# Expert layer of a two-layer encoder: each group's highest expert last, and half of the experts' rows read back during the last two blocks

## The reference

```python
xn = rms_norm(x, norm1)
[q|k|v|q_idx|k_idx|w_idx|u|v_s|g_a|g_b] = xn @ W_in
h = x + (sigmoid(g_a) * (attention @ w_pa) + sigmoid(g_b) * (sgu @ w_pb)) @ w_out
# hier_moe(rms_norm(h)): 4 groups of 8 experts, hidden width 128
g_w, g_idx = top_k(softmax(xf @ w_rg + b_rg), 1)           # one group per token
e_w, e_idx = top_k(softmax(logits of that group), 2)       # two experts in the group
out = sum over the two experts of gate * ((silu(xf @ w_eg) * (xf @ w_eu)) @ w_ed)
y = h + out                                                # next layer, or the final RMSNorm
```

## Time and profile before

| | |
|---|---|
| runs, median (lowest to highest) | 1464.19 us (1463.33 to 1464.4) |
| the profiled execution's own time | 1469.72 us |
| its span in the trace | 1468.0 us |
| PE busy | 1323.0 us, 90% |
| DVE busy | 541.5 us, 37% |
| ACT / POOL busy | 342.6 us, 23% / 219.7 us, 15% |
| DMA moved | 205.63 MB, mean 140 GB/s |
| mean granted TensorE clock | 0.952 |

### The profile page before, as it was taken

One profiled execution on the slowest core, in us unless ns is written; L12 is line 12 of the kernel. 1 busy time (PEld: TensorE's weight loads), 2 busy tenths in 40 slices (PEclk: granted clock), 3 DMA queues, 4 the chain that ended last, 5 costly groups with the idle time before them and its releaser, 6 DMA issues.

```text
span 1468.0 us, 15494 instructions
## 1 busy us (share of the span) xinstructions
PE 1323.0 (90%) x5756; PEld 733.9 (50%) x5756; DVE 541.5 (37%) x1542; ACT 342.6 (23%) x773; POOL 219.7 (15%) x304
## 2 busy tenths in 40 slices
PE   7999898999999996998599989899999999979790
PEld 5654345544444555655385544464444445556450
DVE  1278885100111236321244779831011103452115
ACT  2232466200000100222213325651000010112121
POOL 5011033000000001223240200600000000013313
PEclk9999999999999997999799999999999999979895
DMA  8302102502403316799571110042060060279966
GB/s 237 115 13 59 58 1 70 172 0 70 145 0 121 152 43 227 300 407 392 206 203 58 50 47 34 8 131 104 0 215 0 0 258 29 86 279 410 405 261 237
DMA packets 95485, 205.63 MB, mean 140 GB/s; under 512 B 26465, under 2 KB 35905, under 8 KB 95409
## 3 DMA queue, kind: packets, MB, share of 16 engines
q1 hardware_dynamic: 80800, 178.13, 34.3%
q0 software_dynamic: 14608, 26.49, 5.1%
HBM read 196.29 MB, written 27.78 MB: 153 GB/s over the span
## 4 chain that ended last, share of the span: by engine, by line
PE 81%; DVE 5%; issue 4%; ACT 4%; DMA 3%; PEld 2%; PEldq 1%; POOL 0%; SPq 0%; POOLq 0%; ACTq 0%; DVEq 0%
PE bank L747 34%; PE bank L1029 9%; PE bank L1080 9%; PE bank L1126 8%; PE bank L1137 4%; PE bank L780 3%; PE bank L1113 2%; DMA uv<-xd,mb 2%; PE bank L829 1%; DVE stat L1687 1%; PE bank L1046 1%; PE bank L733 1%; PE bank L933 1%; PE bank L833 1%; DVE x L1821 1%
## 5 line engine op out<-in xcount | busy, mean ns | idle before, releaser
L747 PE MATMUL bank<-ring,xt 128*128 128x512 f32 (+1 forms) x1120 | 434.6, 545 | 7.5 <-DMA ring<-in_w_in 4.5
L747 PEld LDWEIGHTS bank<-ring,xt 128*128 128x128 f32 x1120 | 214.6, 194 | 209.5 <-issue 189.8
L1756 DVE TENSOR_TENSOR scr<-scr,bank 128x512 f32<-128x512 f32 x20 | 13.8, 688 | 368.8 <-PE bank L1029 368.8
L1080 PE MATMUL bank<-ring,xt 128*128 128x512 f32 x320 | 141.3, 594 | 0.0
L541 POOL TENSOR_SCALAR stat<-stat 128x1 f32<-128x1 f32 (+1 forms) x27 | 10.3, 381 | 805.8 <-ACT uv L1213 617.0
L1357 ACT ACTIVATE scr<-bank,stat 128x512 f32<-128x512 f32 x40 | 25.3, 684 | 348.0 <-PE bank L747 348.0
L1080 PEld LDWEIGHTS bank<-ring,xt 128*128 128x128 f32 x320 | 59.3, 190 | 67.0 <-issue 67.0
L780 PE MATMUL bank<-ring,xt 128*128 128x512 f32 x160 | 75.9, 608 | 0.0
L1029 PE MATMUL bank<-ring,att 128*128 128x512 f32 x160 | 72.5, 596 | 2.2 <-ACT sgt L1349 1.8
L1029 PE MATMUL bank<-ring,sgt 128*128 128x512 f32 x160 | 71.9, 592 | 0.0
L747 PE MATMUL bank<-more,xt 128*128 128x512 f32 x160 | 70.3, 592 | 0.0
(11 more groups left out here) (285 smaller groups left out, 1848.7 us busy)
## 6 DMA issues: line engine op xcount, KB each, us to landing
ring<-in_w_in SPq DMA_DIRECT2D x12, 2048.0 KB, 9.2
ring<-in_w_ed SPq DMA_DIRECT2D x32, 512.0 KB, 16.7
ring<-in_w_eg SPq DMA_DIRECT2D x26, 512.0 KB, 10.8
ring<-in_w_eu SPq DMA_DIRECT2D x26, 512.0 KB, 16.8
ring<-in_w_out SPq DMA_DIRECT2D x4, 2048.0 KB, 12.5
more<-in_w_ed SPq DMA_DIRECT2D x14, 512.0 KB, 9.7
qkv<-in_w_eg SPq DMA_DIRECT2D x12, 512.0 KB, 6.3
qkv<-in_w_eu SPq DMA_DIRECT2D x12, 512.0 KB, 7.7
```

The lines of the kernel that those rows point to most:

```text
L747: mm = pe.matmul(out, xt[:, k, t * P:(t + 1) * P], rhs[:, k, :], start=(k == 0), stop=(k == KD - 1))
L1080: mm = pe.matmul(banks[5 + n % 3][:, :], xt[:, k, t * P:(t + 1) * P], w[:, k, :], start=(k == 0), stop=(k == KD - 1))
```

## The change

The experts are renumbered for the blocks: 28 of them (the first seven of each group) in order, then the four that are the highest of their groups. These four fill the last two blocks, b = 15 and 16, and so these blocks write no row of half k = 1. That half is complete once the scatter of block 14 has landed.

SP therefore waits for the scatters of blocks 0 to 14 only, reads half k = 1 (5 DMAs of 512 KB, into the space of `qkv`), then handles the branch for further rows, waits for all scatters, and reads half k = 0 (5 DMAs). DVE adds half k = 1 to x within the blocks' loop: tiles 0 and 1 after `hidden_rows` of block 15, tiles 2 to 4 after that of block 16 (`first_of`). `combine` then has one operation for each tile.

Two further edits belong to it: once, in the first layer, POOL copies the inputs over half k = 1 of `yd` (DRAM to DRAM, 2.6 MB), and waits for that before the first gather; and the final norm's gain is loaded to another place. Only the core of the diff is shown.

```diff
+REST_AT = (0, 8)
+EXPERT_OF = [e for e in range(EXPERTS) if e % NE < NE - 1] + [e for e in range(EXPERTS) if e % NE == NE - 1]
...
-        fin_gain = qkv_flat[:, 2048:2048 + D]
+        fin_gain = more[:, 3072:3072 + D]
...
-        pairs = [w.rearrange("p (k c) -> p k c", k=2) for w in
-                 (uv_flat[:, 0:2048], uv_flat[:, 2048:4096], sgt_flat[:, 512:2560], more[:, 0:2048], more[:, 2048:4096])]
+        last_rows = [uv_flat[:, D * t:D * t + D] for t in range(PT)] + [more[:, 0:D]]
+        first_rows = [qkv[:, t, 0:D] for t in range(NT)]
...
@@ SP, behind the last load of expert weights
+                if L + 1 < DEPTH:
+                    sp.wait_ge(y_psum[L], RING_FREE)
+                    key_columns(L + 1)
+                else:
+                    sp.wait_ge(y_psum[L], RING_FREE)
+                    sp.dma_start(fin_gain, a["final_norm"].partition_broadcast(P)).then_inc(s_gain, 16)
+                by_pair = yd.rearrange("(k t p) c -> k t p c", k=2, t=NT)
+                for z in range(YBUF):
+                    sp.wait_ge(y_out[z], scatters(z) * L + 16 * len(range(z, OVER_AT + 1, YBUF)))
+                for t in range(NT):
+                    sp.dma_start(first_rows[t], by_pair[1, t]).then_inc(combine_in[t][1], 16)
                 sp.wait_ge(experts_known, prior("experts_known", L) + 1)
                 with sp.If(sp.value_load(over_count[:, 0:1], min_val=0, max_val=OVER) != 0):
...
                 for z in range(YBUF):
                     sp.wait_ge(y_out[z], scatters(z) * L + scatters(z))
                 for t in range(NT):
-                    for k in range(2):
-                        sp.dma_start(pairs[t][:, k, :], yd.rearrange("(k t p) c -> t k p c", k=2, t=NT)[t, k]
-                                     ).then_inc(combine_in[t][k], 16)
+                    sp.dma_start(last_rows[t], by_pair[0, t]).then_inc(combine_in[t][0], 16)
...
@@ POOL, behind the loads of the router's weights
+                if L == 0:
+                    pool.dma_start(yd[ROWS:ROWS + SEQ, :], a["x_prompt"][0]).then_inc(yd_set, 16)
+                    pool.dma_start(yd[ROWS + SEQ:2 * ROWS, :], a["x_sample"].rearrange("b t d -> (b t) d")).then_inc(yd_set, 16)
...
+                pool.wait_ge(yd_set, 32)
                 for b in range(XBUF):
...
@@ DVE
+                def first_of(t):
+                    then(V.scalar_tensor_tensor(first_rows[t], first_rows[t], pair_at[:, 2, t, 1:2], x[:, t, :],
+                                                ALU.mult, ALU.add))
+
                 for b in range(NB):
                     hidden_rows(b, b % XBUF, b % 2)
                     if b + 2 < NB:
                         rows_out(b + 2, b % 2)
+                    if b >= NB - 2:
+                        for t in (range(2), range(2, NT))[b - NB + 2]:
+                            dve.wait_ge(combine_in[t][1], 16 * L + 16)
+                            first_of(t)
...
                 def combine(t):
-                    for k in range(2):
-                        dve.wait_ge(combine_in[t][k], 16 * L + 16)
-                        ins = V.scalar_tensor_tensor(x[:, t, :], pairs[t][:, k, :], pair_at[:, 2, t, k:k + 1], x[:, t, :],
-                                                     ALU.mult, ALU.add)
-                        if k == 0:
-                            then(ins)
-                    ins.then_inc(x_new, 1)
+                    dve.wait_ge(combine_in[t][0], 16 * L + 16)
+                    V.scalar_tensor_tensor(x[:, t, :], last_rows[t], pair_at[:, 2, t, 0:1], first_rows[t],
+                                           ALU.mult, ALU.add).then_inc(x_new, 1)
```

More of the change, by code:

```diff
@@ L429, in _ @@
                         sp.wait_ge(rows_sent, prior("rows_sent", L) + 1)
-                        expert(1, EXPERTS * L + 1)
+                        expert(1, EXPERTS * L + EXPERT_OF[1])
                     if u == QU:
@@ L481, in _ @@
                     sp.wait_ge(unit_done, prior("unit_done", L) + done)
-                    expert(e, EXPERTS * L + e)
+                    expert(e, EXPERTS * L + EXPERT_OF[e])
                 sp.wait_ge(mt_done, prior("mt_done", L) + 2 * NT)
-                expert(10, EXPERTS * L + 10)
+                expert(10, EXPERTS * L + EXPERT_OF[10])
                 for t in range(NT - 1):
@@ L487, in _ @@
                 sp.wait_ge(unit_done, prior("unit_done", L) + 15)
-                expert(5, EXPERTS * L + 5)
+                expert(5, EXPERTS * L + EXPERT_OF[5])
                 rows_kept(NT - 1)
@@ L493, in _ @@
                 for e in (6, 7):
-                    expert(e, EXPERTS * L + e)
+                    expert(e, EXPERTS * L + EXPERT_OF[e])
                 sp.wait_ge(r_psum, prior("r_psum", L) + NT)
-                expert(9, EXPERTS * L + 9)
+                expert(9, EXPERTS * L + EXPERT_OF[9])
                 for e in range(PLACES, 2 * NB, 2):
@@ L510, in _ @@
                             row = sp.value_load(over_expert[:, bass.ds(2 * v + (ALWAYS + h), 1)], min_val=0, max_val=EXPERTS - 1)
-                            expert_up(h, EXPERTS * L + row, over_w[L])
-                            expert_down(h, EXPERTS * L + row, over_w[L])
+                            expert_up(REST_AT[h], EXPERTS * L + row, over_w[L])
+                            expert_down(REST_AT[h], EXPERTS * L + row, over_w[L])
                     sp.wait_ge(y_over, earlier(sp) + (16 * REST + 16))
[L514 to L521, removed]
+                    for t in range(NT):
+                        sp.dma_start(first_rows[t], by_pair[1, t]).then_inc(over_w[L], 16)
                 for z in range(YBUF):
@@ L1200, in _ @@
                         pe.wait_ge(h_done[L], b)
-                        up(places[0:2], 0)
+                        up([places[i] for i in REST_AT], 0)
                         pe.wait_ge(h_done[L], b + 1)
@@ L1206, in _ @@
                         pe.wait_ge(y_ready[L], b)
-                        down(places[0:2], 0)
+                        down([places[i] for i in REST_AT], 0)
         @block.scalar
@@ L1510, in tile_route @@
                                     ALU.add).then_inc(chosen_ready, 1)
-                then(V.tensor_tensor(number[:, t, :], chosen[:, t, :], ids[:, 1:EXPERTS + 1], ALU.mult))
+                then(V.tensor_tensor(number[:, t, :], chosen[:, t, :], ids[:, BR + 2 * NT:], ALU.mult))
                 V.tensor_reduce(number_k[:, t, 0:1], number[:, t, :], AX.X, ALU.max)
@@ L1816, in _ @@
                         hidden_rows(v + NB, 0, 0)
[L1818 to L1825 removed]
+                    dve.wait_ge(over_w[L], 96 * REST + 16 * NT)
+                    for t in range(NT):
+                        ins = V.scalar_tensor_tensor(first_rows[t], first_rows[t], pair_at[:, 2, t, 1:2], x[:, t, :],
+                                                     ALU.mult, ALU.add)
+                    ins.then_inc(xin_ready[L], 1)
+                    dve.wait_ge(xin_ready[L], 2 * (NB + REST) + 1)
+                def combine(t):
+                    dve.wait_ge(combine_in[t][0], 16 * L + 16)
+                    V.scalar_tensor_tensor(x[:, t, :], last_rows[t], pair_at[:, 2, t, 0:1], first_rows[t],
+                                           ALU.mult, ALU.add).then_inc(x_new, 1)
                 def finish(t):
@@ L1867, in _ids @@
     pairs = 1 + np.arange(2 * ROWS).reshape(2, NT, P).transpose(2, 1, 0).reshape(P, 2 * NT)
-    return np.concatenate([np.tile(np.arange(BR), (P, 1)), pairs], axis=1).astype(np.float32)
+    units = 1 + np.argsort(EXPERT_OF)
+    return np.concatenate([np.tile(np.arange(BR), (P, 1)), pairs, np.tile(units, (P, 1))], axis=1).astype(np.float32)
 def kernel(**inputs):
```

10 lines of the change are left out of this document (5 added, 5 removed).

## The result

The changed kernel took 1469.64 us in the median of nine runs (1466.13 to 1474.55), the kernel before 1463.33 on the same chip: ratio 1.0044 with a 95% interval of [1.0027, 1.006], 6.3 us slower. Forecast were +7.4 and 1471.6. The profiled execution took 1468.33, its span is 1466.6.

A forecast was written before the change was run, and what follows sets the result against it. PE was taken to bound the kernel, with 81% of the chain. Landing lateness 13.6 minus gains 1.8 and 4.4 gave +7.4 us on 1464.19, so 1471.6 us, 0.5% slower; range +0.5 to +10, 1465 to 1474.

The forecast's parts named there:

- Block 16's product late by 5.2 and 7.0 us behind two `first_of`: On DVE, `hidden_rows` of block 16 queues behind two operations awaiting reads: 5.2 us late in layer one, 7.0 in two.
- the 3.7 that I had named as a sign of being wrong: Block 14's scatter landing earlier than 3.7 us after its issue would show the prediction wrong.
- 1.2 absorbed: Between `hidden_rows` and down(16), the step shrinks from 2.7 to 1.5 us, giving back 1.2 of the lateness.
- Half clock, +1.9 each: After PE's wait, down(16) runs at half clock, 1.96 us becoming 3.9: +1.9 in each layer.
- Last scatter +13.6 in all: Landing of each layer's last scatter: 5.9 us late in the first, 7.7 in the second, +13.6 together.
- Given back in the first layer 1.8: From last landing to PE's projection: one read and operation fewer ahead, start about 9.3 us behind instead of 11.2, gain 1.8.
- Given back in the second layer 4.4: From last landing to last `finish`: ten DVE operations instead of 15, 19.4 us instead of 23.8, gain 4.4.
- the two ends that I had named: Second layer's end: all five tiles at POOL's slow pace gain 1.8 us; with no contention, the full 7.4.
- Copy, places, renumbering 0: DRAM copy hidden, 0 (if not, up to 5 us); renumbering 0, block 16's DMA waits under 1; new places 0.
- faster, since the wait is off the path: Rival at block 16's `hidden_rows`: product on time, only the tails count, -6.2 us, 1458; chance 0.10.
- More than this wait: Rival: copy delays weights, or (second half) scatters of blocks 15 and 16 land slower among reads; +10 to +13; chance 0.13.
- The wait costs less: Rival: no clock penalty and second layer's end near its floor; +1 to +2.5 us, 1465 to 1466.5; chance 0.20.

The follow-up runs named there:

- e1: Changed kernel with all five `first_of` behind block 16's product, none ahead; 1461.68 us, ratio 0.9995 to the kernel before.
- e7: The kernel before, unchanged, run again for a second trace; 1462.91 us.
- e10: The changed kernel run again unchanged; 1469.83 us, ratio 1.0032 to the kernel before.
- e6: Changed kernel plus 48 unused PE transposes ahead of across(16), to fill PE's wait; 1468.38 us, ratio 1.0037 to the kernel before.
- e2: Changed kernel's expert order, copy and places, but both halves read behind the last scatter; 1463.96 us, ratio 1.0005 to the kernel before.
- e9: Two tiles read early, all `first_of` behind block 16's product, plus 88 unused PE transposes starting layer two; 1458.34 us, ratio 0.995 to the kernel before.
- e12: Kernel before plus 98 unused PE transposes at the second layer's start; 1465.23 us, ratio 1.0002 to the kernel before.
- e3: Changed kernel with early reads in the first layer only; 1468.27 us, ratio 1.0037 to the kernel before.
- e4: Changed kernel with early reads in the second layer only; 1466.36 us, ratio 1.0023 to the kernel before.
- e5: Changed kernel with only tiles 0 and 1 read early, all `first_of` behind block 16's product; 1457.72 us, ratio 0.9977 to the kernel before.
- e8: Changed kernel with one `first_of` instead of two ahead of block 16's product; 1465.48 us, ratio 1.0006 to the kernel before.
- e11: Second run of the changed kernel with one `first_of` ahead of block 16's product; 1467.48 us, ratio 1.0012 to the kernel before.

## Why the prediction was right, step by step

- **Block 16's product late by 5.2 and 7.0 us behind two `first_of`: the mechanism is shown.** e1 moves nothing but these operations, and the delay and the slowdown go. Sizes, from the table, against e7: 6.4 and 6.4 us (e10: 6.1 and 7.3). Two errors offset each other there, by luck. The path through DRAM was shorter: from the issue of scatter 14 to the end of the second `first_of` 10.5 and 9.4 us, where I had 11.4 and 10.4, since the first data came 3.3 us behind the landing instead of 4.0 and 3.7, and the scatter took 4.45 and 2.83 instead of 4.7 and 3.7. The 2.83 lies below the 3.7 that I had named as a sign of being wrong. And the time that it is measured against was too late: from scatter 14 to block 16's product the first trace had 6.2 us in the first layer, with 2.08 of wait and a cold PE in it, e7 has 4.1 (second layer 3.4 and 3.1).
- **1.2 absorbed: 1.4.** From `hidden_rows` to down(16) 712.36 - 711.11 = 1.25 us, and as much in the second layer, where e7 has 2.7.
- **Half clock, +1.9 each: +1.5 and +1.7** (3.49 and 3.70 against 1.96). e6 shows it by taking it away in the second layer. The Trainium skill's rule in "TensorE: Matmul & The Clock Gate", section "HAM oscillation — how this bites in real kernels", that a wait for a DMA drops the clock for the burst behind it, agrees with these rows.
- **Last scatter +13.6 in all: +13.2 and +13.6** (changed and e10 against e7: 6.5 + 6.7 and 6.1 + 7.5).
- **Given back in the first layer 1.8: too small.** From landing to the third tile's transposes 15.5 us in e7, 11.9 in the changed kernel and 12.0 in e10: 3.5. Of this, 2.9 is the start of the projection, 8.2 us behind the landing where I had 9.3 (e7 11.1): the first data came 3.5 behind it instead of 4.0, and the 16 transposes ran in one piece (3.56 us) instead of 1.97 and 1.95 with 0.67 between them. The other 0.6 is the clock: the projection ran at full clock throughout, 3.89 against 4.51 in e7. I had put 0.1 for the clock the other way, between a start 1.9 earlier and a gain of 1.8; no run shows that term.
- **Given back in the second layer 4.4: 3.6 and 3.2.** I had forecast the end 19.4 us behind the landing, and it is 19.6 and 20.0; e7 needs 23.2 there, not 23.8. POOL's roots set the pace, between the two ends that I had named, all slow and none slow.
- **Copy, places, renumbering 0: e2 shows it** for the three together. The renumbering did change something that I had ruled out as "under 1": with the new order the step to block 16 lasts 5.7 to 6.0 us in every kernel that does nothing early ahead of it but e9's first layer (6.5), with the old one 7.3 to 9.4 in the first layer and 6.3 to 6.6 in the second. Whether that is how block 16's weights arrive was not tried.
- **The sum.** 13.2 - 3.5 - 3.6 = +6.1, and 13.6 - 3.5 - 3.2 = +6.9 for e10, where +7.4 was forecast and +6.3 measured. That the total comes out so near is in part luck: the first layer's gain was 1.7 too small, the second's 0.8 to 1.2 too large, and the last landing was up to 0.4 less late than forecast. The range had a slip too: with all of its terms at their lower ends, 7.4 - 3.8 - 3.0 - 1.0 is -0.4, not +0.5. The profiled execution of before was no typical one, as I had allowed for: over these two stretches alone it is 4.5 us longer than e7, so that subtracting the first trace from the trace after would have given +1.5. e7 as the base is backed by e12, which is the kernel before up to the last scatter: its landings are 17.0 and 16.1, e7's 17.1 and 16.2.

Of the rivals, "faster, since the wait is off the path" fell with e1, e3 and e4. "More than this wait" was wrong for the changed kernel, where the last scatter took its 3.2 us, since the reads are done by then; its second half, a scatter slow among the reads, is what happened in e1. "The wait costs less" asked for a PE that keeps its clock, and down(16) took 3.49 and 3.70. The branch for further rows was not taken: the changed kernel too has 34 scatters. My theory of e1, that a product on time would leave the tails' gain of about 6, fell on it.

## What to carry to other kernels

Work that is pulled forward must not stand in an in-order queue ahead of something that the critical path waits for, if its own input arrives later than that something: ask what stands behind each new wait. Two of five tiles read early, and added behind the critical product, gave the gain that five read early lost, because a scatter on the path goes slower while bulk reads are under way. And take the base of a difference from more than one trace: the single wait of 2 us that happened to be in mine was as large as the terms that I was summing.

## What the runs showed of the hardware that I had not expected

- An indirect scatter of one block landed in 3.2 us alone. With five reads of 512 KB issued 5.2 and 6.4 us ahead of it, it took 7.22 and 6.02; with two, which were through by then, 3.81 and 3.23.
- A part of such a scatter is its issue on GpSimd: 0.97 us with VectorE idle, 1.28 to 1.84 where a `first_of` was already running (e1, e5, e8, e9, e11). In e11's second layer, where the `first_of` began 0.37 us after the issue, it was 0.97 again. But for e1, where the reads add their part, the landing moved by the same amount.
- The length of the gap ahead of it does not alone tell at which clock PE works on. e7 kept 1.00 through a gap of 1.15 us ahead of down(16); in e12 the clock was at 0.50 after gaps of 0.88 and 2.11 us in short order, and in e6 it fell within 2 us after one of 1.43 (its windows). What ran ahead differed too: down products in e7, transposes in e6 and e12.

```profile
712.00:714.00 2.00, 0.50 (x3) 0.31 (x5) 1.04 (x2) 0.28 (x1) 0.00 (x0) 1.00 0.93 358
714.00:716.00 2.00, 2.00 (x6) 0.50 (x6) 1.45 (x2) 0.00 (x0) 0.00 (x0) 0.54 0.86 346
```

- GpSimd's root operations on 128x1 elements take 0.19 and 0.57 us with VectorE idle (before, at 499 us), and mostly 1.28 and 1.39 beside VectorE's operations on 128x1024, about as long as one of those (1.28). With half of the additions gone, they and not VectorE set the pace of the last five tiles. How they fall varies from one execution to the next: the same kernel needed 20.0 us from the last landing to its end in e8 and 17.7 in e11.
